# First attention stage: VectorE copies the turned probabilities, and scales a head's values one head later

## The reference

```python
def even_mixer(x, w_in, b_f, sinks, w_o):
    qa, ka, va, qb, kb, vb, fg = split_cols(x @ w_in, EVEN_SIZES)
    ...
    out_a = sliding_window_sink_attention(qa, ka, va, sinks)   # softmax(q k^T + bias, with a sink) v
    out_b = causal_block_attention(qb, kb, vb, log_f)          # softmax(q k^T + forget bias) v
    return jnp.concatenate([out_a, out_b], axis=-1) @ w_o
```

## Time and profile before

| What | us |
|---|---|
| median of 3 runs | 2344.25 |
| lowest and highest of them | 2342.65, 2346.51 |
| the profiled execution | 2347.36 |
| its span in the profile | 2345.6 |

### The profile page before, as it was taken

The page is one execution under the profiler, slowest core; times in us unless marked ns, Lnnn a source line. Parts: engine busy times, 40 slices in busy tenths (PEclk is TensorE's granted clock), DMA queues, the critical chain, the costliest instruction groups (busy, mean ns, idle before and its releaser), DMA issues.

```text
span 2345.6 us, 33786 instructions
## 1 busy us (share of the span) xinstructions
PE 2227.9 (95%) x13726; PEld 1970.9 (84%) x13726; DVE 1709.8 (73%) x2149; ACT 1175.8 (50%) x1404; POOL 235.2 (10%) x183
## 2 busy tenths in 40 slices
PE   7899999998899999997999989899999999989998
PEld 7778888888678888886998988799989988867998
DVE  4667678995667679997877885777787775586555
ACT  3554356784654356884334674433343344534333
POOL 5200312312000312310000011000000020000000
PEclk9899999998999999998999999999999999999999
DMA  9128778995028778996886323488778843306652
GB/s 250 60 96 332 252 267 309 352 354 186 23 96 328 250 263 317 363 350 216 291 275 217 146 98 118 142 291 289 245 244 278 271 153 135 109 1 210 194 180 72
DMA packets 241451, 505.56 MB, mean 216 GB/s; under 512 B 10383, under 2 KB 104529, under 8 KB 241296
## 3 DMA queue, kind: packets, MB, share of 16 engines
q1 hardware_dynamic: 216144, 417.84, 51.0%
q10 hardware_dynamic: 21600, 77.09, 9.2%
q0 software_dynamic: 3552, 8.47, 1.5%
HBM read 502.31 MB, written 1.05 MB: 215 GB/s over the span
## 4 chain that ended last, share of the span: by engine, by line
PE 62%; DVE 9%; ACT 2%; issue 1%; DMA 0%; DVEq 0%; ACTq 0%
PE PS L1104 21%; PE PS L1120 10%; PE PS L939 7%; PE PS L1211 6%; PE PS L897 4%; PE PS L1310 2%; PE PS L1330 2%; PE PS L1220 1%; DVE WGL L2384 1%; PE PS L1374 1%; DVE AR L2387 1%; PE PS L1591 1%; PE PS L1406 1%; PE PS L865 1%; DVE AR L2384 0%
## 5 line engine op out<-in xcount | busy, mean ns | idle before, releaser
L2384 DVE TENSOR_TENSOR WGL<-ring,WGH 128x2048 fp32r<-128x2048 f32 (+1 forms) x291 | 599.6, 2069 | 232.1 <-ACT WGH L1812 121.5
L1104 PE MATMUL PS<-XTB,WGH 128*128 128x256 f32 x2816 | 513.0, 284 | 0.3
L1104 PEld LDWEIGHTS PS<-XTB,WGH 128*128 128x128 f32 x2816 | 445.2, 192 | 10.1 <-issue 3.0
L1104 PE MATMUL PS<-XTB,WGL 128*128 128x256 f32 x1408 | 398.6, 283 | 0.0
L1104 PEld LDWEIGHTS PS<-XTB,WGL 128*128 128x128 f32 x1408 | 270.1, 192 | 0.0
L1812 ACT ACTIVATE WGH<-ring 128x1024 fp32r<-128x1024 f32 (+2 forms) x107 | 145.1, 1361 | 184.2 <-PE PS L939 62.0
L1979 ACT ACTIVATE WGH<-ring 128x2048 fp32r<-128x2048 f32 x96 | 183.3, 1914 | 102.7 <-PE PS L1211 39.6
L2384 DVE TENSOR_TENSOR WDL<-ring,WDH 128x1024 fp32r<-128x1024 f32 (+1 forms) x128 | 207.1, 1618 | 24.2 <-ACT WDH L1979 24.1
L2023 ACT ACTIVATE XN<-PS 128x256 f32<-128x256 f32 x88 | 33.8, 384 | 372.6 <-PE PS L1104 368.3
L939 PE MATMUL PS<-XTB,WGH 128*128 128x256 f32 x1088 | 207.7, 292 | 10.3 <-DVE WGL L2384 5.8
L939 PEld LDWEIGHTS PS<-XTB,WGH 128*128 128x128 f32 x1088 | 174.3, 196 | 21.0 <-issue 12.2
(11 more groups left out here) (529 smaller groups left out, 4472.1 us busy)
## 6 DMA issues: line engine op xcount, KB each, us to landing
FA<-in_ada_w ACTq DMA_DIRECT2D x144, 512.0 KB, 6.2
ring<-in_moe_w_up SPq DMA_DIRECT2D x64, 1024.0 KB, 7.0
ring<-in_moe_w_gate SPq DMA_DIRECT2D x64, 1024.0 KB, 7.6
ring<-in_moe_w_down SPq DMA_DIRECT2D x64, 1024.0 KB, 7.5
ring<-in_ffn_w_gate SPq DMA_DIRECT2D x44, 1024.0 KB, 5.8
ring<-in_ffn_w_up SPq DMA_DIRECT2D x44, 1024.0 KB, 10.4
ring<-in_ffn_w_down SPq DMA_DIRECT2D x44, 1024.0 KB, 7.4
ring<-in_hyb_w_in SPq DMA_DIRECT2D x10, 1152.0 KB, 7.5
```

Source lines behind the costliest of these rows:

```text
L1104: ins = mm(PS[:, 4 + b, m * T:(m + 1) * T], w_[:, b, w], x_[:, k, :], start=k == 0 and q == 0, stop=k == KD - 1 and q == 2)
L2384: return V.tensor_tensor(out_, x_, y_, op)
```

## The change

VectorE takes over the copy of the turned probabilities in the "even" stage, and in that stage the scaling of a head's values moves one round later. In the new order VectorE's round i is: reciprocal of head i-2, logits of head i, copy for head i-2, scaling of head i-3. A wait on `o`, raised by its own scaling, stands before the addition and the reciprocal, since the reciprocal of head i-2 goes to the buffer that the scaling of head i-4 reads. ScalarE keeps the copy in the "odd" stage only. TensorE's program is unchanged.

```diff
--- before.py
+++ after.py
@@ ScalarE, attention @@
                     if i in first:
                         copies(first[i])
-                    if i >= 2:
+                    if i >= 2 and r.name == "odd":
                         u, b = r.ub + i - 2, i % 2
                         act.wait_ge(S("pt_ps"), u + 1)
                         if u >= 2:
@@ VectorE, attention @@
                 n = len(units)
-                for i in range(n + 2):
-                    if i >= 2:
+                late = 3 if r.name == "even" else 2
+                for i in range(n + late):
+                    if 2 <= i < n + 2:
 
                         u, w, b = r.ub + i - 2, units[i - 2], i % 2
+                        if late == 3 and u >= 2:
+                            dve.wait_ge(S("o"), u - 1)
                         dve.wait_ge(S("p"), 2 * (u + 1))
                         if w.kind == "window":
                             c(tt(SM[:, b, :], SM[:, b, :], ES[:, b, :], ALU.add))
...
                     if beside:
                         beside(i)
-                    if i >= 2:
-
-                        u, w, b = r.ub + i - 2, units[i - 2], i % 2
+                    if r.name == "even" and 2 <= i < n + 2:
+
+                        u, b = r.ub + i - 2, i % 2
+                        dve.wait_ge(S("pt_ps"), u + 1)
+                        if u >= 2:
+                            dve.wait_ge(S("o_ps"), u - 1)
+                        V.tensor_copy(PT[:, b, :], PS[:, 4 + b, 0:MW]).then_inc(S("pt"), 1)
+                    if i >= late:
+
+                        u, w, b = r.ub + i - late, units[i - late], (i - late) % 2
                         dve.wait_ge(S("o_ps"), u + 1)
                         tt(XN[:, :, w.at:w.at + HD], PS[:, 6 + b, 0:2 * HD].rearrange("p (t d) -> p t d", t=TT),
                            bc(RC[:, b, :].unsqueeze(2), (P, TT, HD))).then_inc(S("o"), 1)
```

## The result

The changed kernel takes 2353.12 us (median of 8 runs) against 2345.23 for the kernel before in the same comparison: 1.0032 times as long, 95% interval 1.0022 to 1.0042, some 7.9 us. The forecast was 2355.5, range 2350.5 to 2368. As a difference it was 11.0 us, so the level came nearer (2.4 off) than the difference did (3.1 off). That is luck in part: the kernel before, 2344.25 when the forecast was made, is 1.0 us slower in this comparison. The profiled execution took 2353.25 us, with a span of 2351.5.

A forecast was written before the change was run, and what follows sets the result against it. The prediction took waits between TensorE and ScalarE, with no engine full, to bound the stage. The change would close a ring: 10.8 us more over thirteen steps plus 0.2 at the end, 11.0, giving 2355.5 us, range 2350.5 to 2368.

The forecast's parts named there:

- The ring: Attention stage: logits, copy, values and next scores wait on each other through VectorE and TensorE; 13 steps 44.23 against 33.40 us.
- Its terms: Hand-overs and operations summed per step at full clock: fox 2.95 us, 3.39 with transposes; window 3.07 to 3.51.
- The eleven steps from head 4 on: Steps from the scores of head 4 to those of head 15, all priced at the full clock.
- The first two steps: Head 2 to 3 and 3 to 4, priced at the half clock: 5.10 and 4.22 us.
- The rival that the clock would rise later than 96: Stage start: half clock some heads longer, 1.15 us more a step; clock rival's chance 0.27, including a renewed drop.
- its other half, that the clock drops again: Within the stage: 1.15 us more a step; three to eight heads 2358 to 2366 (0.17), all eleven steps 2371 (0.10).
- The end of the stage: From the scores of head 15 to the mark letting TensorE go on: 5.7 us for 5.52, 0.2 more.
- The sum: Whole stage: 10.8 us more in the thirteen steps and 0.2 at the end, 11.0, all passed on.
- The faster side: Rival: the ring is not closed, relieving ScalarE opens the stage, TensorE bounds next; 3.4 us gain, 2341; chance 0.05.
- TensorE's room of 6.7 us: In the faster rival: TensorE busy 15.97 of 20 us, so at best a fifth of the stage's 33.4 us.
- the 13 steps: From the scores of head 2 to those of head 15: 33.40 us before, 44.23 forecast.
- No delay came back later: Answers the no-change rival: stage slower but the time comes back later in the kernel; chance 0.03.

The follow-up runs named there:

- cutting it on VectorE's side: Changed kernel with VectorE's copy for head i-2 ahead of the logits of head i; 0.9958 of the kernel before, 0.9979 in a later comparison.
- on TensorE's: Changed kernel with TensorE issuing the values of a head one round later, behind the next head's scores; 0.9959 of the kernel before.
- the scaling three times: Changed kernel with each scaling made three times, behind the copy on VectorE; 1.0058 of the kernel before.
- the scaling not late: Changed kernel with the scaling in its old round, the copy still on VectorE behind the logits; 1.0051 of the kernel before.
- the doubled copy: Changed kernel with VectorE's copy made twice, the second raising the semaphore; 1.0116 of the kernel before.
- the late scaling alone: Changed kernel with the copy back on ScalarE in both stages, the scaling still one round later; 0.9996 of the kernel before.
- the changed kernel again: The changed kernel, unaltered, measured and profiled a second time; 1.0037 of the kernel before.

## Why the prediction was right, by its steps

**The ring** was the reason, and the experiments show it: cutting it on VectorE's side or on TensorE's makes the kernel faster than before, by the steps from head 4 on as well (34.1 us with the ring, 23.0 and 20.9 without, 25.6 before); lengthening the copy in it lengthens each step by the copy; work of the same length just outside of it leaves the steps alone; the late scaling by itself does nothing.

**Its terms**, forecast and measured: scores to logits 1.01 and 1.01 (0.96 when transposes of queries and keys stand before the scores); logits 0.64 and 0.56, as the copy starts together with the last read of the accumulator; copy 0.54 and 0.55; to the values 0.05 and 0.06; values to scores 0.71 and 0.71; transposes 0.44 and 0.44. The eleven steps from head 4 on: 34.91 and 34.12 (96.47 to 130.59).

**The first two steps** were the term that was mis-sized: 5.10 and 4.22 forecast, 4.07 and 2.97 measured. I had let the clock rise at 96 us as before; it rose near 92, and near 87 in the second profile of the same kernel, where these steps were 3.48 and 2.97:

```profile
86.00:88.00 2.00, 1.51 (x6) 0.79 (x4) 1.21 (x7) 0.76 (x4) 0.00 (x0) 0.63 0.02 4
88.00:90.00 2.00, 1.28 (x7) 0.83 (x7) 0.65 (x5) 1.97 (x9) 0.00 (x0) 1.00 0.00 0
```

In two neighbours, the scaling three times and the scaling not late, it did rise at 96, as I had assumed. There the steps were 5.11 and 3.63, and 5.09 and 3.63: the first is my term. The second is 0.6 under it, because the rise fell into that step and I had priced all of it at the half clock. The rival that the clock would rise later than 96 was the wrong way round for this kernel, and its other half, that the clock drops again, came true only with the doubled copy. Nothing in the prediction foresaw the earlier rise.

**The end of the stage**: 0.2 us more forecast, 0.1 measured up to the transposes (5.56 and 5.62). That these would then run at the full clock I had not forecast; it gives back 1.1 us.

**The sum**, from the first scores to the output product: 11.0 forecast, 6.2 in the profiles. The difference is 2.3 in the two steps, 0.8 in the others, 0.1 at the end, 1.1 in the transposes, and 0.5 between the first scores and those of head 2, again the clock. The medians say 7.9. What lies between 6.2 and 7.9 isn't settled: executions of one kernel differ by 7 us and more (2342.65 to 2349.92 before, 2346.73 to 2354.99 after), and one profile of each can't share that out. The profile of the kernel before is one with a late rise of the clock and half-clock transposes; whether its other executions are like it no run shows.

**The rivals.** The faster side needed the ring to be open, and the change closes it. Where it was cut, the gain was 5 to 10 us rather than the 3.4 I gave it. I had halved TensorE's room of 6.7 us for hand-overs; with the values behind the next scores the 13 steps lost 7.3 (33.40 to 26.06). Of these 4.75 are in the eleven steps at the full clock, 25.61 to 20.86, and there a fifth would be 5.1: so the busy share of the earlier trace rows was a fair floor, and for this order I should not have halved it. The other 2.6 are in the two steps after head 2, where the clock rose near 93 us instead of 96. With the copy ahead of the logits the eleven steps lost 2.6, about the half. The Trainium skill (Perfetto Trace Analysis, Identifying the Most-Contended Engine) says to optimize the engine with the highest occupancy first. In the earlier trace rows that is ScalarE, by 16.00 us to TensorE's 15.97. But less work for that engine is not what decided: with the copy taken off it the kernel was slower with the ring closed and faster with the ring cut, and moving the copy within ScalarE's own order, at the same load, made it faster as well. No delay came back later in the kernel: from the output product to the end of the span it is 2213.1 us before and 2211.6 after, and between 2204.8 and 2213.1 in all fourteen profiles, with no relation to the length of the stage.

## What to carry to other kernels

When work moves to another engine, draw what then stands in front of it and behind it in that engine's fixed order, and look for a ring through the engines; its length is the period, however idle all of them are, when it is longer than each engine's own work. A ring is cut by reordering, which cost nothing in these runs: here the same copy was worth +0.3% behind the logits and -0.2 to -0.4% in front of them. And judge such an experiment by the steps in its profile, not by the time alone: the tripled scaling had its rival's time and not its rival's cause.

## What was unexpected of the hardware

TensorE's clock moved more than the schedules did. With the doubled copy the two-level clock fell in the middle of the stage, where TensorE was busy 4.15 us of 8 before it, and stayed at 1.2 GHz for over 40 us although TensorE, now slower, was then busy 6.17 of 8. In the changed kernel it held at 1.00 with 13.97 of 20. At the start of the stage it rose near 92 us in one profile of the changed kernel and near 87 in the other, and near 96 in the profile before; with the late scaling alone it rose near 87, fell near 91 and rose again near 97. The result's transposes took 1.96 to 1.97 us in seven of the fourteen profiles and 3.37 to 3.68 in the other seven, without an order that explains it. Between the changed kernel again and the one with the scaling three times these two places make 3.7 us: 2.6 from the scores of head 0 to those of head 4 (11.25 and 13.85), and 1.1 from the transposes to the output product.
